# A hybrid decoder step on one core: the last four experts written out, and the end of the expert stage reordered

## What is computed

```python
h = h + mix                                    # token mixers
m = rmsnorm(h, prm['norm_moe_g'])
h = h + moe(m, ...)                            # top 4 of 32 experts
gate = jax.nn.sigmoid(rmsnorm(h, prm['norm_ple_g']) @ prm['w_ple_gate'])
h = h + (p @ prm['w_ple_proj']) * gate
# one expert, on its tokens:
h = x[tok] @ w_up[e] + b_up[e]                 # 1024 x 2048
gate = jnp.minimum(h[:, ::2], 7.0)
lin = jnp.clip(h[:, 1::2], -7.0, 7.0)
act = gate * jax.nn.sigmoid(1.702 * gate) * (lin + 1)
y = (act @ w_down[e] + b_down[e]) * g[:, None] # 1024 x 1024, added to the tokens' rows
```

## Time and profile before

| | |
|---|---|
| median of 3 runs | 1130.45 us (1130.18 to 1134.32) |
| the profiled execution | 1131.03 us, its span 1129.3 us |
| PE busy | 1086.0 us, 96% |
| DVE, ACT, POOL busy | 34%, 14%, 3% |
| read from memory | 429.03 MB, 384 GB/s over the span |
| granted PE clock, mean | 0.997 |

### The profile page before, as it was taken

The page is one execution under the profiler, slowest core; times in us unless marked ns, Lnnn a source line. Parts: engine busy times, 40 slices in busy tenths (PEclk is TensorE's granted clock), DMA queues, the critical chain, the costliest instruction groups (busy, mean ns, idle before and its releaser), DMA issues.

```text
span 1129.3 us, 16240 instructions
## 1 busy us (share of the span) xinstructions
PE 1086.0 (96%) x6475; PEld 450.5 (40%) x6478; DVE 380.6 (34%) x969; ACT 162.2 (14%) x365; POOL 33.7 (3%) x80
## 2 busy tenths in 40 slices
PE   9999999999999999989898899999999999999897
PEld 6763444333333333333333243434333324343344
DVE  3866665232222222222131222322313222222165
ACT  2543232000000000000001010101010100010023
POOL 2300130000000000000000000000000000000000
PEclk9999999999999999999999999999999999999999
DMA  9833968999999999999999999999999999999951
GB/s 297 297 132 112 372 247 342 431 424 431 429 431 427 431 431 431 433 429 435 429 431 432 428 422 433 431 428 429 429 431 435 429 429 427 427 428 428 428 208 43
DMA packets 34580, 433.87 MB, mean 384 GB/s; under 512 B 5337, under 2 KB 6497, under 8 KB 16366
## 3 DMA queue, kind: packets, MB, share of 16 engines
q1 hardware_dynamic: 32880, 428.47, 90.3%
q0 software_dynamic: 1456, 4.48, 1.2%
q10 hardware_dynamic: 206, 0.40, 0.1%
HBM read 429.03 MB, written 4.30 MB: 384 GB/s over the span
## 4 chain that ended last, share of the span: by engine, by line
PE 70%; DMA 24%; DVE 3%; ACT 2%; issue 1%; SPq 0%; DVEq 0%; ACTq 0%
PE bank L1108 28%; DMA ring<-in_w_up_dram 24%; PE bank L1156 14%; PE bank L1090 6%; PE bank L666 5%; PE bank L788 3%; PE bank L1069 3%; PE bank L690 1%; PE bank L1140 1%; DVE arena L1663 1%; PE bank L1185 1%; DMA ring<-in_w_in_dram 1%; PE bank L980 1%; PE bank L1066 1%; PE bank L1146 1%
## 5 line engine op out<-in xcount | busy, mean ns | idle before, releaser
L1108 PE MATMUL bank<-ring,aT 128*64 128x512 f32 x1536 | 345.4, 597 | 24.6 <-DMA ring<-in_w_up_dram 24.6
L1108 PEld LDWEIGHTS bank<-ring,aT 128*64 128x64 f32 x1536 | 107.2, 137 | 245.9 <-issue 211.0
L1156 PE MATMUL bank<-ring,arena 128*64 128x512 f32 x768 | 169.6, 594 | 0.2
L2090 DVE TENSOR_TENSOR h<-h,bank 128x512 f32<-128x512 f32 (+1 forms) x90 | 61.3, 684 | 181.2 <-PE bank L1090 179.4
L1108 PE MATMUL bank<-arena,aT 128*64 128x512 f32 x512 | 114.8, 595 | 0.0
L2116 DVE COPY aT<-bank 64x512 f32<-64x512 f32 x32 | 22.2, 694 | 244.8 <-PE bank L1156 244.8
L1470 ACT ACTIVATE arena<-arena 128x256 f32<-128x256 f32 x64 | 26.7, 418 | 537.9 <-DVE arena L2107 537.9
L2107 DVE TENSOR_SCALAR arena<-bank 128x256 f32<-128x256 f32 x64 | 27.2, 425 | 218.7 <-PE bank L1108 217.4
L1156 PEld LDWEIGHTS bank<-ring,arena 128*64 128x64 f32 x768 | 53.8, 137 | 100.9 <-issue 98.2
L1090 PE MATMUL bank<-aT,arena 128*32 128x512 f32 (+1 forms) x180 | 78.3, 622 | 0.0
L1108 PEld LDWEIGHTS bank<-arena,aT 128*64 128x64 f32 x512 | 35.3, 136 | 73.1 <-issue 71.6
(11 more groups left out here) (375 smaller groups left out, 763.9 us busy)
## 6 DMA issues: line engine op xcount, KB each, us to landing
ring<-in_w_up_dram SPq DMA_DIRECT2D x38, 4096.0 KB, 27.8
ring<-in_w_down_dram SPq DMA_DIRECT2D x48, 2048.0 KB, 28.8
arena<-in_w_up_dram SPq DMA_DIRECT2D x13, 4096.0 KB, 29.0
ring<-in_w_up_dram SPq DMA_DIRECT2D x19, 2048.0 KB, 29.4
arena<-in_w_down_dram SPq DMA_DIRECT2D x16, 2048.0 KB, 28.3
arena<-in_w_up_dram SPq DMA_DIRECT2D x6, 2048.0 KB, 30.4
ring<-in_w_in_dram SPq DMA_DIRECT2D x3, 2048.0 KB, 13.8
ring<-in_w_in_dram SPq DMA_DIRECT2D x4, 1024.0 KB, 11.8
```

Of the source, the lines that this page charges most:

```text
L1108: mm = pe.matmul(bank[n][CAP * hf:CAP * hf + CAP, :], xT[:, odd, 2 * j + a, :], up_cols(x, j, a, hf, n), start=False, stop=(j == 3 and a = ...
L1156: mm = pe.matmul(bank[4][CAP * hf:CAP * hf + CAP, :], actT[:, b, t, :], tile_of(x, UP_TILES + t)[:, 1024 * b + 512 * hf:1024 * b + 512 * h ...
L2090: tt(part, part, bank[5 + j % 2][at:at + ROWS[c], :], ALU.add).then_inc(s_free[j % 2], 1)
```

## The change

1. The last body (experts 28 to 31) is taken out of the loop on PE, ACT and DVE and written out with `end=True`. Every engine loads a second register (`n_more`) for it.
2. The last expert gathers nothing and picks nothing.
3. The last two experts are scattered one by one. Expert 30 turns its own selection (slots 0 to 63), and expert 31 runs its five jobs between its own up tiles, from 64 partitions of `gselT` and `ysb`.
4. Expert 31 then turns its selection into both halves of `gselT`; its result goes to `ysb` with columns 0 to 511 in partitions 0 to 63 and 512 to 1023 in 64 to 127. The last scatter takes each half of the columns from its own 64 partitions, in the order `LAST_JOBS`.
5. Expert 31 turns its second half of the activation after the first two down steps.
6. The very last down tile comes as two transfers of 1 MB, the second under a semaphore of its own.
7. After the experts the chunks go in the order 0, 2, 1, and PE starts on chunk 0 with half of the rows of `w_ple_gate` before chunk 1 is turned; DVE's turns stand between its adds. Banks are renamed for it.
8. At the start three small parameter transfers count on the semaphore of seven others, so one wait before the `par` product takes the place of two.

```diff
+        LAST_JOBS, LAST_ORDER = [1, 2, 0, 3, 4], (0, 2, 1)
...
-                fetch(n_more * NE + BODY * last + x, BODY * last + x, x)
+                fetch(n_more * NE + BODY * last + x, BODY * last + x, x, range(N_TILES if x < 3 else N_TILES - 1))
+            final = down_rows(I["w_down"][0][NE - 1], 1).rearrange("p (a n) -> p a n", a=2)
+            sp.wait_ge(S["up_full"], n_more * (2 * NE) + 2 * NE - 2)
+            sp.dma_start(tile_of(3, 5)[:, 0:2048], final[:, 0, :]).then_inc(w_full[buf(3, 5)], 16)
+            sp.dma_start(tile_of(3, 5)[:, 2048:4096], final[:, 1, :]).then_inc(S["last_in"], 16)
...
-            pe.wait_ge(S["par_in"], 16 * 7)
+            pe.wait_ge(S["par_in"], 16 * 10)
...
-            pe.wait_ge(S["pbr_in"], 16 * 3)
```

PE, `scatter` and `expert` (the arguments `slots` and `waited` of `scatter` take the slice of the partitions and leave out the wait):

```diff
+                    if final and j < 3:
+                        if j == 0:
+                            pe.wait_ge(S["ysb_ok"], 4 * m + 3)
+                            pe.wait_ge(s_free[0], S_READS[0] * m + S_BASE)
+                        scatter(m, ((1,), (2, 3), (4,))[j], slice(0, CAP))
+                        if j == 0:
+                            scatter(m, (0,), slice(0, CAP), waited=True)
+                        if j == 2:
+                            turn_selection(i + 2, places + 1)
+
+                if not final:
+                    pe.wait_ge(S["sel_ok"], i + 2)
+                    if first:
+                        pe.wait_ge(S["m3_ok"], 3)
+                    gather(1 - odd)
+                    if odd or single:
+                        turn_selection(i + 1, places + 1)
+
+                def turn_act(n):
                     if n == 0:
                         pe.wait_ge(S["a0_free"], i + 1)
                     else:
...
+
+                turn_act(0)
+                if not final:
+                    turn_act(1)
...
+                    if final and k == 6:
+                        pe.wait_ge(S["last_in"], 16)
                     if k == 2:
-                        pe.wait_ge(S["a1_free"], 3 * m + 2 * odd + 2)
+                        if final:
+                            turn_act(1)
+                        pe.wait_ge(S["a1_free"], places + turns + 2)
```

PE, after the loop:

```diff
+            n_more = pe.value_load(npi[0:1, 1:2], min_val=0, max_val=PASSES - 1)
+            with pe.Fori(MID, n_more * (NE // BODY) + (NE // BODY - 1)) as q:
...
+            for x in range(BODY):
+                expert(n_more * (NE // BODY) + (NE // BODY - 1), x, x % 2 == 0, end=True)
...
+            for j in LAST_JOBS:
+                (c, hf), b = SCATTER[j], LAST_BANK[j]
                 for f in ((hf,) if c < 2 else (0, 1)):
-                    mm = pe.matmul(bank[b][:, :] if c < 2 else bank[b][T_S * f:T_S * f + T_S, :], gselT[:, TOK[c]],
-                                   ysb[:, 512 * f:512 * f + 512], start=True, stop=True)
+                    half = slice(CAP * f, CAP * f + CAP)
+                    mm = pe.matmul(bank[b][:, :] if c < 2 else bank[b][T_S * f:T_S * f + T_S, :], gselT[half, TOK[c]],
+                                   ysb[half, 0:512], start=True, stop=True)
                 mm.then_inc(s_full[j % 2], 1)
...
+            def turn_last(n):
+                c = LAST_ORDER[n]
...
+            turn_last(0)
+            turn_last(1)
+            stored(pe, ("nT", 0, 0))
+            pe.wait_ge(pw_in[0], 16)
+            rows_product("pg", 0, w_pg, range(4), last=False, halves=(0,))
+            turn_last(2)
+            rows_product("pg", 0, w_pg, range(4), last=False, halves=(1,))
+            rows_turned(2)
+            rows_product("pg", 2, w_pg, range(4), last=False, split=True)
+            rows_turned(0)
+            pe.wait_ge(pw_in[1], 16)
+            rows_product("pg", 2, w_pg, range(4, 8), first=False, split=True)
+            rows_product("pg", 0, w_pg, range(4, 8), first=False)
+            rows_turned(1)
+            rows_product("pg", 1, w_pg, halves=(0,))
```

ACT, `expert`, and DVE:

```diff
+                def selection_out():
+                    act.wait_ge(S["a1_full"], places + 1)
+                    act.activation(gselT, bank[7][:, 0:T], ACT.Copy).then_inc(S["a1_free"], 1)
+
+                if final:
+                    selection_out()
...
+                if single or odd and not final:
+                    selection_out()
...
+                if final:
+                    act.activation(ysb[0:CAP, 0:512], bank[4][0:CAP, :], ACT.Copy).then_inc(S["ysb_ok"], 1)
```

```diff
+                if final:
+                    tt(gsel[:, :, 0:CAP], sel[:, odd, :, :],
+                       gate_t[:, :, bass.ds(i, 1)].to_broadcast([P, NCH, CAP]), ALU.mult).then_inc(S["g_ok"], 1)
+                    add_pair(m)
...
+                if final:
+                    dve.tensor_copy(ysb[CAP:2 * CAP, 0:512], bank[4][CAP:2 * CAP, :]).then_inc(S["ysb_ok"], 1)
...
+            for j in LAST_JOBS[0:3]:
+                add_last(j)
+            turned("nT", 7, [(0, 0)])
+            for j in LAST_JOBS[3:5]:
+                add_last(j)
+            turned("nT", 7, [(2, 0), (2, 1), (0, 1), (1, 0), (1, 1)])
```

More of the change, by code:

```diff
@@ L1080, in landed, with scatter @@
                 return 16 * (nth(q, x, j) + (1 if in_halves else 0))
-            def scatter(m, jobs):
+            def scatter(m, jobs, slots=slice(0, 2 * CAP), waited=False):
                 for j in jobs:
@@ L1086, in scatter, with turn_selection, expert @@
                     before = scatter_reads(j - 2) if j >= 2 else 0
-                    pe.wait_ge(s_free[j % 2], S_READS[j % 2] * m + before + S_BASE)
+                    if not waited:
+                        pe.wait_ge(s_free[j % 2], S_READS[j % 2] * m + before + S_BASE)
                     o = bank[5 + j % 2]
                     for f in ((hf,) if c < 2 else (0, 1)):
-                        mm = pe.matmul(o[:, :] if c < 2 else o[T_S * f:T_S * f + T_S, :], gselT[:, TOK[c]],
-                                       ysb[:, 512 * f:512 * f + 512], start=True, stop=True)
+                        mm = pe.matmul(o[:, :] if c < 2 else o[T_S * f:T_S * f + T_S, :], gselT[slots, TOK[c]],
+                                       ysb[slots, 512 * f:512 * f + 512], start=True, stop=True)
                     mm.then_inc(s_full[j % 2], 1)
-            def expert(q, x, add_before, first=False):
+            def turn_selection(gates, places):
+                pe.wait_ge(S["g_ok"], gates)
+                pe.wait_ge(S["a1_free"], places)
+                for c in range(NCH):
+                    mm = pe.transpose(bank[7][:, TOK[c]], gsel[0:ROWS[c], c, :], ident[0:ROWS[c], 0:ROWS[c]])
+                mm.then_inc(S["a1_full"], 1)
+            def expert(q, x, add_before, first=False, end=False):
                 i, m, odd = BODY * q + x, 2 * q + x // 2, x % 2
+                single, final = end and x == BODY - 2, end and x == BODY - 1
+                places = 3 * m + odd + (1 if final else 0)
+                turns = 1 if odd or single else 0
                 if not first:
@@ L1209, in _, with rows_turned @@
                 transposed(("nT", c, 1), h, c, 4)
-            for c in ORDER:
+            def rows_turned(c):
                 stored(pe, ("nT", c, 0))
                 stored(pe, ("nT", c, 1))
-                if c == 2:
-                    pe.wait_ge(pw_in[0], 16)
-                    rows_product("pg", 2, w_pg, range(4), last=False, split=True)
-                    pe.wait_ge(pw_in[1], 16)
-                    rows_product("pg", 2, w_pg, range(4, 8), first=False, split=True)
-                else:
-                    rows_product("pg", c, w_pg, halves=(0, 1) if c == 0 else (0,))
+            turn_last(0)
[13 more added lines that the diff above has]
+            rows_product("pg", 1, w_pg, halves=(0,))
             for n in range(2):
@@ L1462, in _, with expert @@
                 act.sem_inc(sem, 1)
-            def expert(q, x):
+            def expert(q, x, end=False):
                 i, m, odd = BODY * q + x, 2 * q + x // 2, x % 2
+                single, final = end and x == BODY - 2, end and x == BODY - 1
+                places = 3 * m + odd + (1 if final else 0)
+                turns = 1 if odd or single else 0
+                def selection_out():
[3 more added lines that the diff above has]
+                    selection_out()
                 act.wait_ge(S["act_ready"], 2 * i + 1)
@@ L1501, in _ @@
             act.wait_ge(S["npass_ok"], 2)
-            n_pass = act.value_load(npi[0:1, 0:1], min_val=1, max_val=PASSES)
-            with act.Fori(MID, n_pass * (NE // BODY)) as q:
+            n_more = act.value_load(npi[0:1, 1:2], min_val=0, max_val=PASSES - 1)
+            with act.Fori(MID, n_more * (NE // BODY) + (NE // BODY - 1)) as q:
                 for x in range(BODY):
                     expert(q, x)
+            for x in range(BODY):
+                expert(n_more * (NE // BODY) + (NE // BODY - 1), x, end=True)
             jt = view(3072, D)
-            for n, c in enumerate(ORDER):
+            for n, c in enumerate(LAST_ORDER):
                 r = slice(0, ROWS[c])
```

(7 more changed lines are left out.)

65 lines of the change are left out of this document (27 added, 38 removed).

## The result

The change is slower by a little: 1133.39 us median (20 runs, 1131.44 to 1135.54 but for one disturbed one) against 1131.67 us for the kernel before (20 runs, 1129.96 to 1134.32). The ratio is 1.0017, 95% interval 1.0010 to 1.0023, so 1.9 us (1.1 to 2.6), far inside the 0.5% that the forecast called no change, and yet not zero. The profiled execution took 1134.46 us (span 1132.7), 3.4 us above that of before; this one execution is an unlucky one: it is the latest of the eight in the table further on.

A forecast was written before the change was run, and what follows sets the result against it. Weight transfers were taken to bound the kernel up to expert 31's last up tile (1068.5 us), PE from there on. Terms +2.8 - 1.3 - 1.4 = +0.1 us gave 1130.5 us, no change; range 1127.3 to 1133.5.

The forecast's parts named there:

- Expert 30, one turn more: Expert 30 turns and copies out its own selection, so expert 31 starts its first up tile 0.75 us later.
- Expert 31, five jobs between the up tiles: In expert 31, five scatter jobs from 64 partitions cost the full 5.01 us, as from 128; lower bound half.
- the rival in which the scatter hides: In expert 31, 64 partitions cost half, the fourth up tile is late by 0.3 us: 1128 us; chance 0.15.
- 2.8 us are left over.: At expert 31's fourth up tile, the waits for weights are used up and it starts 2.8 us later than before.
- From the last up tile to the end of its down product: In expert 31, the down product ends 9.5 us behind the last up tile's end (U), before 10.8: gain 1.3 us.
- From the down product to the first gate product: After the experts, the first gate product starts at 5.5 us, DVE's adds setting that start; gain 1.4 us.
- VectorE's gate work, the register load and the joined wait: Gate work at the end, second load in the middle section, parameter wait at the start: no cost in the sum.
- Slower: Straight code of the written-out last four experts slows each; from 1.5 us an expert, 6 us, 1137 us; chance 0.04.

The follow-up runs named there:

- control: The change unaltered, timed once more beside the kernel before: 1133.52 us, ratio 1.0018.
- pair: The change with the last two experts scattered as a pair again, without one-by-one scatter and row groups: 1131.03 us, ratio 0.9996 to the kernel before.
- count: The change with VectorE's wait of the final adds counted in the order in which the jobs now come: 1132.54 us, ratio 1.0007 to the kernel before.
- before_load: The kernel before with a second register load on TensorE and VectorE and nothing else: 1132.25 us, ratio 1.0001.
- peel_only: The kernel before with its last loop body written out on TensorE, ScalarE and VectorE, and the second register load: 1132.96 us, ratio 1.0013.
- peel_b: peel_only timed once more, the same edit to the kernel before: 1133.23 us, ratio 1.0013.
- change_late28: The change with twelve dummy products (2.6 us) in expert 28: 1133.99 us, ratio 1.0017 to the kernel before.
- pair_2us: pair with 12 dummy products (2.6 us) spread over expert 31's first three up tiles: 1133.03 us, ratio 1.0003 to the kernel before.

## Why the prediction was wrong, step by step

The sum was +0.1 us, and the change costs 1.9. The range up to 1133.5 held the median, narrowly. Of the 2.9 us between 1130.5 and 1133.39, 1.2 belong to the reference: three runs of the kernel before gave 1130.45, all later ones 1131.7.

- **"Expert 30, one turn more", +0.75.** Right. Expert 30 took 30.5 us in `control` and 29.8 before, 0.7 more.
- **"Expert 31, five jobs between the up tiles", full price.** Right, 2.10, 1.98 and 1.12 us. Partitions in use do not change the time of a product here: the rule of the Trainium skill ("TensorE: Matmul & The Clock Gate", "Why this matters for your kernels") holds, and the rival in which the scatter hides falls. It spoke against this part of the change, and without that part (`pair`) the kernel is 2.4 us faster.
- **"2.8 us are left over."** Right as to kind and nearly as to size: 2.4 us on the mean over eight executions, 1.9 to 3.3 in single ones.
- **"From the last up tile to the end of its down product", U + 9.5.** Right: 1087.41 - 1077.90 = 9.5, in part because two errors cancel. The first down step started at U + 1.25 and not U + 1.55, and the last six steps took 5.4 us and not 5.16. The gain is 1.2 us, since the tile before ended at 1068.53 + 3.65 = 1072.2. That the halved last transfer gained nothing was not tested by itself; no run lacks it alone.
- **"From the down product to the first gate product", 5.5 us, gain 1.4.** Right as to mechanism, 0.3 us off: 5.85 us, gain 1.1. The step put a pair of jobs in two row groups at 0.86 us, three at 2.6; the three pairs took 3.17. And it read the order of the adds but not the count that they wait for, 0.34 us, of which `count` gives back 0.2 at the end.
- **VectorE's gate work, the register load and the joined wait, 0.** Right as far as the runs show. `before_load` shows no cost of the load, and no run tests the joined wait alone; in the profiles TensorE has no idle time at that product, before or after. VectorE had caught up before its last piece and waited for ACT there:

```profile
1126.27 0.43 DVE L2269 TENSOR_TENSOR arena<-arena 128x256 f32<-128x256 f32 x1 [0.85 <-ACT arena L1602]
```

- **"Slower", from straight code.** This is the step that failed. It looked for a cost of straight code in TensorE's pace, and found none, rightly. The forecast took the landing of the last up tile, 1068.5 us, as given: "Nothing in the change reads fewer weights." It did not ask whether anything is *added* to the queue of transfers that was 100% busy in its own windows row. The straight body's code is, and the sum had this at nothing. `peel_only` and `peel_b` put that edit at 1.5 us, which makes 0.1 + 1.5 = 1.6 of the measured 1.9; all six estimates together put it at 0.9, which makes 1.0.

What stays open: the profiles place 0.6 us in the stream, and the runs put the straight body at 0.9 to 1.5. The intervals, 1 us either way each, allow that the two are the same, and that they are not. If the body costs 0.9, another 0.9 us of the change's loss has no place. Whether a late TensorE adds to the loss in executions that were not profiled could not be told either, since the two kernels with dummies in expert 28 disagree with their profiles.

## What to carry over

Idle time ahead of a transfer is room only for what is put in it, and one execution shows its size for that execution alone. Before you fill it, ask whether what you move there costs more PE time than it takes away behind it: here 6.3 us (0.75, 5.0 and 0.5) moved in, against 3.4 us of waits, and 2.3 came off. Where the DMA engines are full up to the transfer that sets the end, count everything that enters them. Unrolling a loop enters its code. And when work is reordered, check that each wait counts in the new order.

## What was not expected of the hardware

- A code transfer of 16 KB occupied one DMA engine for 1.07 us in the middle of a full weight stream, and the tile under way landed up to 1.5 us late (`change_late28`: 6.4 us behind the one before it, instead of 4.9; `pair_2us`: 6.3); in other executions the same transfers cost nothing.
- Two row groups of 64 partitions did not halve the time. Six pairs of records took 3.17 us, 0.53 a pair. Before, twelve records took 4.68 us; the last seven of them started 0.43 us apart, so two one behind the other take 0.86.
- The granted clock falls for a few us in some executions right after TensorE has waited for weights. In the first execution of the change it fell behind a wait of 2.13 us, and the windows row shows 0.77 as the mean over 7 us, part of it at 2.4 GHz and part at 1.2:

```profile
951.00:958.00 7.00, 4.87 (x16) 1.46 (x16) 0.00 (x0) 0.00 (x0) 0.00 (x0) 0.77 0.99 424
```

  The 24 records from 953.48 us on took 7.07 us, and expert 27 took 28.9 us where it takes 27.2, the 1.7 us that make this execution the latest of the eight. Waits of the same length left the clock at full speed in others.
